# A depthwise convolution and its layer norm in a decoder layer: the taps go in pairs through PSUM, and the norm starts inside the input projection

## The reference, cut to what matters

```python
yp = ffn_half_step(yp, ffn1...)                       # feed-forward 1
q, k, v, u = project_in(rmsnorm(yp, mix_norm), w_in)  # 2560 output columns; u = a * sigmoid(g), 512 channels
o_a = merge_by_denominator([... three dilated windows ...])      # attention of 8 heads
u_ext = pad(u, 30 rows in front)                      # samples: 30 cached rows in front
y = conv_general_dilated(u_ext, conv_w, feature_group_count=512) # 31 taps per channel
o_b = silu(layernorm(y + conv_b, conv_ln_g, conv_ln_b))          # over the 512 channels
x = x + [o_a | o_b] @ w_out
... cross attention, feed-forward 2, final norm
```

## Time and profile before

| | us |
|---|---|
| median of three runs | 2866.34 (2862.71 to 2868.13) |
| the profiled execution | 2870.69 |
| its span in the trace | 2868.9 |
| PE busy | 2648.9 (92%) |
| DVE busy | 1105.5 (39%) |
| ACT busy | 515.9 (18%) |
| POOL busy | 713.8 (25%) |

### The profile page before, as it was taken

One profiled execution on the slowest core, in us unless ns is written; L12 is line 12 of the kernel. 1 busy time (PEld: TensorE's weight loads), 2 busy tenths in 40 slices (PEclk: granted clock), 3 DMA queues, 4 the chain that ended last, 5 costly groups with the idle time before them and its releaser, 6 DMA issues.

```text
span 2868.9 us, 44329 instructions
## 1 busy us (share of the span) xinstructions
PE 2648.9 (92%) x16847; PEld 2478.7 (86%) x16847; DVE 1105.5 (39%) x2107; ACT 515.9 (18%) x1177; POOL 713.8 (25%) x404
## 2 busy tenths in 40 slices
PE   7999999999998999488988988869899999999998
PEld 7899999999997999366546978739799999999998
DVE  5222222222226799733333141622522222222224
ACT  4200000000003111255222121320300000000002
POOL 6522222222220342022000210102222222222220
PEclk9999999999999999789999999989999999999999
DMA  6311111111110121244984112562111111111101
GB/s 210 118 44 44 44 44 44 44 44 44 44 44 15 45 75 61 90 134 121 282 231 128 44 45 77 192 234 69 37 44 44 44 44 44 44 44 44 44 30 63
DMA packets 215022, 224.81 MB, mean 78 GB/s; under 512 B 11658, under 2 KB 181702, under 8 KB 210851
## 3 DMA queue, kind: packets, MB, share of 16 engines
q1 hardware_dynamic: 197943, 195.58, 22.4%
q10 hardware_dynamic: 17004, 28.21, 2.7%
HBM read 191.10 MB, written 32.67 MB: 78 GB/s over the span
## 4 chain that ended last, share of the span: by engine, by line
PE 75%; issue 9%; DVE 7%; DMA 4%; ACT 2%; PEld 1%; SPq 1%; DVEq 1%; POOL 1%; ACTq 0%; PEldq 0%; POOLq 0%
PE ps L650 21%; PE ps L652 21%; PE ps L651 21%; DVE ya L1787 1%; PE ps L1018 1%; PE ps L974 1%; DVE hidl L1613 1%; PE ps L901 1%; PE ps L912 1%; DVE hl L1579 1%; PE ps L988 1%; DMA Kw<-in_cache_win_k 1%; DMA Vn<-out_new_win_v_sample 1%; PE ps L884 1%; DMA cK<-in_cache_mem_k 1%
## 5 line engine op out<-in xcount | busy, mean ns | idle before, releaser
L650 PE MATMUL ps<-hh,wh 128*128 128x384 f32 (+1 forms) x3168 | 1039.3, 328 | 50.3 <-DVE hl L1579 24.7
L652 PE MATMUL ps<-hl,wh 128*128 128x384 f32 (+1 forms) x3168 | 1037.7, 328 | 0.0
L651 PE MATMUL ps<-hh,wl 128*128 128x384 f32 (+1 forms) x3168 | 1037.6, 328 | 0.0
L650 PEld LDWEIGHTS ps<-hh,wh 128*128 128x128 f32 x3168 | 598.9, 189 | 54.0 <-issue 52.7
L651 PEld LDWEIGHTS ps<-hh,wl 128*128 128x128 f32 x3168 | 599.0, 189 | 0.0
L652 PEld LDWEIGHTS ps<-hl,wh 128*128 128x128 f32 x3168 | 598.6, 189 | 0.0
L595 POOL CAST wh<-raw 128x1024 fp32r<-128x1024 f32 x148 | 161.2, 1089 | 1480.7 <-PE ps L652 1353.0
L1625 DVE TENSOR_TENSOR ht<-ps,sg 128x384 f32<-128x384 f32 x132 | 70.7, 536 | 925.9 <-PE ps L652 924.5
L597 POOL TENSOR_TENSOR wl<-raw,wh 128x1024 fp32r<-128x1024 f32 x148 | 378.5, 2557 | 11.9
L650 PE MATMUL ps<-hidh,bh 128*128 128x384 f32 (+1 forms) x1056 | 346.7, 328 | 11.7 <-DVE x L1637 11.7
L1637 DVE SCALAR_TENSOR_TENSOR x<-ps,x 128x384 f32<-128x384 f32 (+1 forms) x528 | 276.5, 533 | 185.4 <-PE ps L652 184.8
(11 more groups left out here) (226 smaller groups left out, 2103.6 us busy)
## 6 DMA issues: line engine op xcount, KB each, us to landing
raw<-in_ffn_gate SPq DMA_DIRECT2D x44, 512.0 KB, 3.8
raw<-in_ffn_up SPq DMA_DIRECT2D x44, 512.0 KB, 3.8
raw<-in_ffn_down SPq DMA_DIRECT2D x44, 512.0 KB, 3.5
Kw<-in_cache_win_k SPq DMA_DIRECT2D x48, 256.0 KB, 7.4
Vw<-in_cache_win_v SPq DMA_DIRECT2D x48, 256.0 KB
raw<-in_w_in SPq DMA_DIRECT2D x20, 512.0 KB, 3.7
Kw<-in_cache_win_k SPq DMA_DIRECT2D x8, 1024.0 KB, 12.7
Vw<-in_cache_win_v SPq DMA_DIRECT2D x8, 1024.0 KB
```

The source lines that it names most:

```text
L650: pe.matmul(out, w_hi_, a_hi, start=first, stop=False)
L651: pe.matmul(out, w_lo_, a_hi, start=False, stop=False)
L652: return pe.matmul(out, w_hi_, a_lo, start=False, stop=last)
```

## The change

Four things are changed, all between the start of the input projection and the start of the prompt attention.

1. **Taps.** The loop over channel tiles becomes a list, `conv_order`. Only the prompt's 1024 columns are left on DVE. The running sum of a channel tile lies in two PSUM banks (4 and 5 for even tiles, 6 and 7 for odd ones) and goes to `ya` with the last tap. After 14 taps of tile 0 the taps of two tiles alternate: tiles 0 and 2 in one row, 1 and 3 in the other.
2. **Samples.** ACT multiplies the 64 sample columns by each tap (124 small instructions, `tap_samples`) into a tile `tapped`, after the stores of units 8, 9, 12 and 13. DVE adds the 31 products in one reduction for each channel tile.
3. **Layer norm.** PE's last four units are written out of the loop. Behind unit 17 PE makes the channel sums (`ln_mean`), behind unit 19 those of the squares (`ln_sums`). ACT squares behind the store of unit 18, into a tile of its own, one chunk at a time, and does the root and silu before barrier 3. Silu's result goes to `mix` one channel tile at a time.
4. **Barrier 4 is gone.** Engines add to `phase_end` (`arrive`) without waiting. The cache transposes use a PSUM bank for each channel tile. PE waits for the copies to `ucs`, SP for the last unit's stores instead of barrier 3, POOL's `kc` for the arrivals and `vc` for the transfers to `mix`. Tiles are laid out anew so that the early loads lie over nothing that is still in use.

```diff
+    def conv_order():
+        lead = 14
+        ops = [("glu", 0, 0)] + [("tap", 0, t) for t in range(lead)] + [("glu", 1, 0)]
+        one = [("tap", 0, t) for t in range(lead, CONVW)] + [("glu", 2, 0)] + [("tap", 2, t) for t in range(CONVW)]
+        two = [("tap", 1, t) for t in range(CONVW)] + [("sum", 0, 0), ("sum", 1, 0), ("glu", 3, 0)]
+        two += [("tap", 3, t) for t in range(CONVW)]
+        while one or two:
+            ops += one[:1] + two[:1]
+            one, two = one[1:], two[1:]
+        at = ops.index(("tap", 2, CONVW - 1)) + 3
+        return ops[:at] + [("sum", 2, 0)] + ops[at:] + [("sum", 3, 0)]
...
         A = S["pa"]
-        sp.wait_ge(phase_end, 3 * 3)
+        sp.wait_ge(unit_done, SLOTS + COL["w_out"])
+        for w in range(2):
+            sp.wait_ge(S["nm"][f"st{w}"], S["nm"].base[f"st{w}"] + 16 + 8 * 3 * CT)
...
+                        if p == 0 and dst is kc:
+                            pool.wait_ge(phase_end, 3 * 4)
                         if p == 0 and dst is vc:
-                            pool.wait_ge(phase_end, 3 * 4)
+                            pool.wait_ge(S["conv"]["obst"], 16 * CT)
...
+        def ln_mean():
+            pe.wait_ge(C["tap"], CT * CONVW)
+            pe.wait_ge(C["sred"], CT)
+            for c, (c0, n) in enumerate(CHUNKS):
+                for k in range(CT):
+                    mm = pe.matmul(ps[:, LNB[c], 0:n], ones[:], ya[:, k, c0:c0 + n], start=(k == 0), ...)
+                mm.then_inc(C["mean"], 1)
+        def beside_projection(w):
+            if w == 1:
+                ln_mean()
+            if w == 3:
+                ln_sums()
+        proj("w_in", S["nm"], 20, CHUNKS, hh, hl, lambda c: KT * (c + 1), beside_projection)
         barrier(pe, 3)
...
-            if k >= 1:
-                pe.wait_ge(C["ucs"], 2 * k)
-            pe.transpose(ps[0:PAD, 4, 0:P], U[:, k, SEQ:SEQ + PAD], ident[:])
+            pe.transpose(ps[0:PAD, 4 + k, 0:P], U[:, k, SEQ:SEQ + PAD], ident[:])
...
-        barrier(pe, 4)
+        arrive(pe)
         A = S["pa"]
         pe.wait_ge(A["tok_in"], 32)
+        pe.wait_ge(C["ucs"], 2 * CT)
...
+        def tap_samples(k):
+            act.wait_ge(C["glu"], 2 * k + 2)
+            if k >= 2:
+                act.wait_ge(C["sred"], k - 1)
+            for t in range(CONVW):
+                out = tapped[:, k % 2, t, :].rearrange("p (b t) -> p b t", t=TS)
+                ... act.activation(out, Us[:, k, :, t:t + TS], ACT.Copy, scale=taps[:, k, t:t + 1]) ...
+        def ln_squares():
+            for c, (c0, n) in enumerate(CHUNKS):
+                for k in range(CT):
+                    act.wait_ge(C["xc"], c * CT + k + 1)
+                    if c:
+                        act.wait_ge(N["summed"], N.base["summed"] + c)
+                    act.activation(sq_ln[:, k, 0:n], ya[:, k, c0:c0 + n], ACT.Square).then_inc(N["sq"], 1)
+        def ln_end():
+            ... three roots ...
+            for k in range(CT):
+                act.wait_ge(C["ln"], CT * (NC - 1) + k + 1)
+                act.activation(ya[:, k, :], ya[:, k, :], ACT.Silu, bias=...).then_inc(C["ob"], 1)
+                act.wait_ge(C["ob"], k + 1)
+                act.dma_start(mix[(CT + k) * P:(CT + k + 1) * P, :], ya[:, k, :]).then_inc(C["obst"], 16)
+        def store_units(s):
+            for u in range(3 * CT):
+                ... the copies and the store of unit 8 + u ...
+                for k in {0: [0], 1: [1], 4: [2], 5: [3]}.get(u, []):
+                    tap_samples(k)
+                if u == 3 * CT - 2:
+                    ln_squares()
+            for w in range(2):
+                act.wait_ge(s[f"st{w}"], s.base[f"st{w}"] + 8 * 3 * CT + 16)
...
-        store_proj("w_in", S["nm"], stage3, 3 * CT, 2 * CT, z)
+        store_units(S["nm"])
+        ln_end()
         barrier(act, 3)
...
+                bank = 4 + 2 * (k % 2)
+                acc = ps[:, bank:bank + 2, :].rearrange("p b c -> p (b c)")
+                src, dst, w = U[:, k, t:t + SEQ], acc if t < CONVW - 1 else ya[:, k, 0:SEQ], taps[:, k, t:t + 1]
+                ... dve.wait_ge(C["tap"], place["tap", k, t - 1] + 1)
+                ... dve.scalar_tensor_tensor(out=dst, in0=src, scalar=w, in1=acc, op0=ALU.mult, op1=ALU.add)
```

More of the change, by code:

```diff
@@ L397, in rs_bank, with arrive @@
         return 6 + c % 2
+    def arrive(eng):
+        eng.drain().then_inc(phase_end, 1)
     def barrier(eng, n):
@@ L707, in ffn, with proj, four @@
                 groups(FG - 1, beside_last)
-        def proj(name, s, nunits, chunks, ah, al, h_need):
+        def proj(name, s, nunits, chunks, ah, al, h_need, beside_last=None):
             u0 = UNIT[name]
             nc_ = len(chunks)
-            with pe.Fori(0, nunits // 4) as i:
+            def four(i, beside=None):
                 for w in range(4):
@@ L724, in proj @@
                         mm.then_inc(s["part"] if c < nc_ - 1 else unit_done, 1)
+                    if beside is not None:
+                        beside(w)
+            if beside_last is None:
+                with pe.Fori(0, nunits // 4) as i:
+                    four(i)
+            else:
+                with pe.Fori(0, nunits // 4 - 1) as i:
+                    four(i)
+                four(nunits // 4 - 1, beside_last)
         L, Z, C, M = S["load"], S["st"], S["conv"], S["mk"]
@@ L1367, in _ @@
         act.dma_start(new_conv_s, ucs[:, 1:3, :]).then_inc(C["ucst"], 16)
[L1368 to L1383 removed]
+        arrive(act)
         A = S["pa"]
@@ L1789, in _, with sum_samples @@
-        barrier(dve, 3)
-        for k in range(CT):
-            dve.tensor_copy(cct[:, k].rearrange("p a (b t) -> p (a b) t", t=PAD), Us[:, k, :, TS:PAD + TS]
-                            ).then_inc(C["ug"], 1)
+        def sum_samples(k):
+            dve.wait_ge(C["tapped"], CONVW * (k + 1))
+            dve.tensor_reduce(ya[:, k, SEQ:T], tapped[:, k % 2].rearrange("p t c -> p c t"), AX.X, ALU.add
+                              ).then_inc(C["sred"], 1)
+        place = {op: i for i, op in enumerate([op for op in conv_order() if op[0] == "tap"])}
@@ new lines, in _ @@
+        for what, k, t in conv_order():
+            if what == "sum":
+                sum_samples(k)
+            elif what == "glu":
+                dve.wait_ge(S["nm"]["free"], S["nm"].base["free"] + 4 + 2 * NC * (k + 1))
+                dve.tensor_tensor(U[:, k, PAD:PAD + SEQ], U[:, k, PAD:PAD + SEQ], ya[:, k, 0:SEQ], ALU.mult
+                                  ).then_inc(C["glu"], 1)
+                dve.tensor_tensor(Us[:, k, :, PAD:PAD + TS], Us[:, k, :, PAD:PAD + TS],
+                                  ya[:, k, SEQ:T].rearrange("p (b t) -> p b t", t=TS), ALU.mult
+                                  ).then_inc(C["glu"], 1)
+            else:
+                bank = 4 + 2 * (k % 2)
+                acc = ps[:, bank:bank + 2, :].rearrange("p b c -> p (b c)")
+                src, dst, w = U[:, k, t:t + SEQ], acc if t < CONVW - 1 else ya[:, k, 0:SEQ], taps[:, k, t:t + 1]
+                if t == 0:
+                    dve.wait_ge(C["glu"], 2 * k + 2)
+                    dve.tensor_scalar(dst, src, w, vecs[:, V_CB + k:V_CB + k + 1], ALU.mult, ALU.add
+                                      ).then_inc(C["tap"], 1)
+                else:
+                    dve.wait_ge(C["tap"], place["tap", k, t - 1] + 1)
+                    dve.scalar_tensor_tensor(out=dst, in0=src, scalar=w, in1=acc, op0=ALU.mult, op1=ALU.add
+                                             ).then_inc(C["tap"], 1)
@@ L1813, in _ @@
                                          op1=ALU.mult).then_inc(C["ln"], 1)
-        barrier(dve, 4)
+        barrier(dve, 3)
+        for k in range(CT):
+            dve.tensor_copy(cct[:, k].rearrange("p a (b t) -> p (a b) t", t=PAD), Us[:, k, :, TS:PAD + TS]
+                            ).then_inc(C["ug"], 1)
+        arrive(dve)
+        dve.wait_ge(C["ut"], CT)
         A = S["pa"]
```

127 lines of the change are left out of this document (60 added, 67 removed).

## The result

The changed kernel took 2845.65 us in the median of its first four executions (2843.74 to 2857.73), the kernel before 2867.24. The ratio is 0.993 (95% interval 0.9906 to 0.9955). Forecast were 2846, a range of 2839 to 2856, and 0.91 for faster. Session by session the medians differ by 21.6, 19.6 and 19.8 us, and single executions of one kernel scatter by as much.

A forecast was written before the change was run, and what follows sets the result against it. PE was taken to bound the kernel except in a few stretches; shortening 1160.35 to 1224.23 brings attention's first row to 1203.8, -20.4 us. That makes 2850.3 for the profiled execution, 2846 against the median; range 2839 to 2856.

The forecast's parts named there:

- DVE done: Input projection: taps, gate products and sample reductions on DVE sum to an end at 1124.2 us, before 1176.0.
- the first reciprocal to the first silu: Norm's end: this way stays as it was, 12.2 us, so the first silu comes at 1193.5.
- the wait for the store: Norm: ACT newly awaits the last store's landing ahead of the root, 3.3 us, until 1179.5.
- the 384-column row: Taps: the same operation in PSUM at 0.622 us gives 1.04 ns a column and 0.22 us fixed in either memory.
- the prediction's second estimate: Taps: by the skill's table a PSUM source costs 65 ns more a tap, 8 us in all, DVE's end at 1132.
- the prediction's two cases: Sample reductions on DVE: 2.3 us each, or 4.6 each if their stride halves the rate.
- ACT's samples: Narrow taps moved to ACT in the projection: 6.9 us a tile, at the most 15, costing PE nothing.
- The cover: Behind unit 17: DVE is done 12.4 us before PE asks for the last tap; gone at 0.10 us more a tap.
- the clock did not come back sooner: Rival, attention's start: PE's clock returns sooner, up to 4.9 us more gained, 2841 us; chance 0.10.
- half of it given back: Rival, behind the change: something on its own clock does not start earlier, gain only 10 us, 2856; chance 0.07.
- The splits do not stretch a tap: Rival, taps: POOL's splits still stretch them by 2.92 us each, DVE done at 1159.2, time 2869; chance 0.04.
- Reading and writing the same banks: Rival, taps: PSUM reads and writes take turns, 1.07 us more a tap, PE waits 120 us, 2966; chance 0.05.

The follow-up runs named there:

- late_taps: The changed kernel with five more sample reductions on DVE ahead of the last one; ratio to the kernel before 0.9962 (0.9942 to 0.9982).
- second repeat: The changed kernel run a third time, no edit; median 2852.54 us, ratio to the kernel before 0.9921 (0.9895 to 0.9947).
- first repeat: The changed kernel run once more for a second trace, no edit; median 2849.89 us, ratio to the kernel before 0.9933 (0.9907 to 0.9958).

## Why the prediction was right

| step | forecast | measured (first trace) |
|---|---|---|
| DVE done | 1124.2 | 1124.27 |
| PE asks for the last tap | 1136.6 | 1135.16 |
| units 18 and 19 end | 1167.8 | 1166.2 |
| last sum of squares ends | 1176.2 | 1175.5 |
| first reciprocal | 1181.3 | 1179.78 |
| first silu | 1193.5 | 1193.69 |
| barrier 3 passed | 1200.3 | 1200.34 |
| attention's first row | 1203.8 | 1204.19 |
| scores | 1206.8 | 1207.53 |

The mechanism was right at each step. That attention's first row agrees to 0.4 us is partly luck: from the first tap to attention's first row the forecast had 252.0 us (951.8 to 1203.8) and the three traces have 254.0. The squares and their sums took 0.9 us more than forecast, the way from the first reciprocal to the first silu 1.7, the transposes 0.4, and the wait for the store 0.8 less. The first trace's start, 1.5 us early, hid most of the 2.0.

**The taps.** The price from the 384-column row held: 1.29 us a tap, 1.19 from start to start. One step to it was weaker than it reads: a row in PSUM and a wider one in SBUF cannot tell the price a column from the fixed part. The narrow taps of the earlier trace rows close it (0.280 us for 64 columns and 1.285 for 1024 give 1.05 ns a column and 0.21 us fixed, all in SBUF), and so do the runs: 1.290 us in PSUM, 1.285 in SBUF, 5 ns apart and not the 65 of the prediction's second estimate. That the sum in PSUM frees the taps from POOL's splits is shown by putting it back: the splits stretch them again, and with the wait behind unit 17 the gain is gone. DVE's end agrees to 0.1 us partly by luck. The four reductions took 3.73 us each and not 2.3, between the prediction's two cases, 5.7 us too much. Against it, only the gate of tile 1 met a split (2.9 us), the taps were 0.01 us shorter (1 us), and the trace began the convolution 1.5 us early. ACT's samples took 7.8 us a tile (30 multiplications in 7.40 us), where 6.9 to 15 were forecast, and no unit of PE waited for them.

**The cover** of 12.4 us was 10.9 (1135.16 less 1124.27), and `late_taps` found it where it should be. I priced the loss of the cover as idle time alone. Measured, 7.6 us of idle time cost 10.3, since the clock fell.

**The norm.** The new wait for the last stores was priced at 3.3 us, and moving it brought 2.4 (2.79 of idle time in the trace). From the first reciprocal to the first silu it took 13.9 us, not the 12.2 taken over from before. POOL's `qs` copy now fell on DVE's multiplications of the second chunk, which have two SBUF inputs and took 3.94 us instead of 2.21.

**The rivals.** In the first trace and the second repeat the clock did not come back sooner (0.50 in the attention's first 12 us). In the first repeat it did: 0.50 from 1204 to 1210, then 0.82 to 1216, which brought PE about 1 us there, not the 4.9 that the rival was priced at. No loss behind the changed stretch shows: from attention's first row to the end of the span it is 1644.7 us before, and 1651.6, 1638.0 and 1647.5 in the three traces after. The medians' 19.6 to 21.6 us fit the 18.5 of the stretch within their intervals, and half of it given back would not. The splits do not stretch a tap with one input in PSUM. Reading and writing the same banks costs nothing that shows at 1024 columns over two banks.

**What the two parts are worth** the prediction did not say. The taps alone bring 11.9 us, the norm's move the other 6.6. Nor did it say that two units further back the wait would be safe without PSUM.

## What to carry to other kernels

Where VectorE works beside GpSimd, an elementwise chain with its running value in PSUM was free of GpSimd's traffic here, at the same price a column for the form with two tensor inputs. It also freed GpSimd. Before a wait is placed in a full engine's queue, compute when the other side is done, and ask whether a later place costs anything: here the later one was as fast, with 24 us more of cover. Past the cover PE lost the idle time and 2.0 to 2.9 us on top, for waits of 4.2 to 14.9 us. To compare traces, count from the first instruction of the changed code: here that brought a scatter of 1.7 us down to 0.03. A stage bound by transfers can differ by more from one execution to the next than a change brings, so read a small gain at the changed place and not from one total.

## What the hardware showed unexpectedly

- A GpSimd cast of 1.04 us was held for 36.16 us beside VectorE instructions with two SBUF inputs that followed each other without a gap (it began 4.4 us into a row of 32, and ended 2.2 us behind it). In the same work in another order, with each instruction waiting for the one just before it, no cast took over 2.10 us. Why later alternating taps in the same run did let POOL in, and stretched, stays open.
- A VectorE reduction of 31 x 64 fp32 products from SBUF took 3.73 us with a stride of 256 bytes, and 2.21 without.
- A ScalarE multiplication of 64 columns from SBUF took 0.34 us, more than the copy of 64 columns from PSUM (0.22), and 0.40 with a strided output. In a row of 30 one started every 0.25 us.
- A VectorE tap that waited for the one just before it started 1.32 us after it (13 in 17.19 us), one that waited for the last but one 1.19 us.
- PE's clock was down after 7.6 us without work, 0.66 over the next 7.3 us, and after 4.2 us without work, 0.77 over the next 7.4 us.
